# A transformer pair on one Trainium2 core: when the statistic bank is taken again, transposes of first-half weights ahead, and another order for two attention groups

## The chip, the core and the metric

The kernel runs on one core of a Trainium2 chip. The core has five engines with a queue each: TensorE (PE: matmuls, and PEld for its weight loads), VectorE (DVE), ScalarE (ACT), GpSimd (POOL) and SyncE (SP, which issues the DMAs here). Every engine works its own instructions in order; between engines there are semaphores only. The metric is the device time of one launch in microseconds.

## The reference

Two small networks run one after the other on 512 tokens of width 1024, in float32. The first is a block of chunked attention with a relative bias, a gated convolution and an output projection. The second has two layers: sparse top-k attention beside gated linear attention with a squared-ReLU MLP, then stick-breaking attention with another such MLP. The change sits mostly in the stick-breaking layer, whose core is:

```python
def mixer_c(n, w_in, gq, gk, w_out):
    q, k, v = _split(n @ w_in, (C_WIDTH, C_WIDTH, C_WIDTH))
    q = rmsnorm_2(q.reshape(bsz, s_len, N_HEADS_C, HEAD_DIM), gq)   # 8 heads of 128
    k = rmsnorm_2(k.reshape(bsz, s_len, N_HEADS_C, HEAD_DIM), gk)
    ...
    return stick_breaking(q, k, v).reshape(bsz, s_len, C_WIDTH) @ w_out

# stick_breaking, for each head and each block of 128 queries:
    z = q @ k.T * d_h ** -0.5
    lo = where(mask, log_sigmoid(-z), 0.0)
    rc = cumsum(lo, reverse=True)
    a = where(mask, exp(log_sigmoid(z) + (rc - lo)), 0.0)
    out = a @ v
```

## The kernel before

**Precision.** Each float32 matmul operand is split into a high part and a low rest, and three matmuls (high by high, low by high, high by low) add up in one PSUM bank: lines 614 to 616, in `three`. A weight tile (`raw`, 128 x 2048 for each partition row) is split by ACT (line 1401 copies the high part to `wh`) and then by DVE (line 2237 subtracts for `wl`). There are two slots of `raw`, `wh` and `wl`, and `w_lo` counts the finished tiles.

**The stick-breaking layer** is written out by hand as four groups of two heads (`attention_group("stick", g, ...)`, once for each engine) and a closing group 4. Group g projects six blocks from three weight tiles: blocks 0 to 3 are query and key of its two heads (24 matmuls of 512 columns each, banks G0 and G1 in turn), blocks 4 and 5 the values (48 matmuls of 256 columns). Between these blocks PE places the scores, the transposes ("turns") and the products with the values ("av") of the heads of the group before. In group 0 the blocks 0 to 3 run in `first_stick_blocks`, interleaved with the end of the MLP, so that this group has only blocks 4 and 5 left to cover the work of DVE and ACT on its four query and key blocks.

**One query or key block** passes four engines. ACT copies the bank to `tmp` (line 1410) and squares it (line 1418, the high part); POOL makes the exact square (line 2203) and its low rest (line 2208); PE adds over the partitions by two matmuls with ones into the one bank ST (`head_stat`, lines 688 and 689; I call these sums 8 to 23 after their keys); DVE reads ST and makes the mean square (line 2281, `st_x` is raised); ACT takes log, exp and square (lines 1424 to 1426); DVE does a Newton step and scales (lines 2271, 2272, 2772) and raises `st_applied` by a copy of one word (line 2285). `head_stat` waits for the low rest (`sq_low`) and, before the change, for `st_applied` of the sum before it. The copy of block n + 2 into `tmp` waits for `st_applied` of sum n, since there are two buffers.

**The weights of a head** (`weights` on DVE, `softplus` and `exponential` on ACT) come in two halves: score tiles 0 to 2 (banks C0 and C1) and tile 3 (bank C2). ACT: absolute value, exp, log (lines 1718 to 1722); DVE: maximum and add (2829), a reverse scan for each tile (2834), a subtraction (2839), which frees the score bank; ACT: exp (1731), which raises `a_ready`. Then PE transposes ten 128 x 128 pieces into the same three banks (`turns`, line 723), ACT copies them out (1461), POOL masks the diagonals (2197) and PE multiplies by the values (line 1086).

## Time and profile before

| | |
|---|---|
| median of 3 runs | 1581.42 us (1581.22 to 1582.18) |
| profiled execution, its own time | 1582.57 us |
| its span, first to last instruction | 1580.7 us (so 1.9 us lie around it) |
| PE busy | 1561.3 us, 99% |
| DVE, ACT, POOL busy | 1030.1, 725.4, 678.8 us |
| mean granted TensorE clock | 0.998 |

PE is busy nearly all the time; of DVE, ACT and POOL idle time means little except where PE waits for them. In the rows below a timeline row has the start in us from the span's start, the duration in us, engine, line, operation, output and inputs, shape, how many records are merged in it, and in brackets the idle time of the engine before it with what ended that. The duration of a matmul includes its way through the array: unhindered matmuls of 512 columns start 0.23 us apart and last 0.39, so that an idle time in brackets is 0.16 us shorter than what the wait costs (for 256 columns, 0.12 apart and 0.28 long, the same 0.16).

### The profile page before, as it was taken

What the parts mean: (1) busy time and instruction counts of PE and PEld (TensorE: products, weight loads), DVE (VectorE), ACT (ScalarE), POOL (GpSimd) and SP (SyncE); (2) the same over time, 40 slices, a digit from 0 to 9 for tenths busy, and PEclk for the clock granted to TensorE, in tenths of its full rate; (3) what the DMA queues carried; (4) which work ended last, traced back from release to release, by engine and by line L of the source; (5) the groups of instructions that cost most, each with busy time, mean ns of one, the idle gap of its engine ahead of it and who ended that gap; (6) DMA issues with size and microseconds to landing.
All of it is one profiled execution on the core that took longest, in us unless ns stands there. A gap on an engine that the chain in (4) does not pass through costs nothing.

```text
span 1580.7 us, 20565 instructions
## 1 busy us (share of the span) xinstructions
PE 1561.3 (99%) x7578; PEld 1281.5 (81%) x7578; DVE 1030.1 (65%) x1341; ACT 725.4 (46%) x1085; POOL 678.8 (43%) x668
## 2 busy tenths in 40 slices
PE   9999999999999999999999999998999999999999
PEld 7888787787778998888888888777886888888887
DVE  7424554675678977458584848767777557574847
ACT  6323433325245665434353435476765453444433
POOL 0002120104345353285666657432333574857574
PEclk9999999999999999999999999999999999999999
DMA  7232222232311221323233231212120414141321
GB/s 245 80 107 80 80 80 80 96 107 80 104 57 54 93 65 68 136 81 113 101 106 107 82 131 31 99 58 80 54 81 30 158 54 160 53 155 59 134 80 54
DMA packets 25731, 145.07 MB, mean 92 GB/s; under 512 B 3936, under 2 KB 5680, under 8 KB 9264
## 3 DMA queue, kind: packets, MB, share of 16 engines
q1 hardware_dynamic: 25648, 143.95, 26.4%
q8 instruction: 53, 0.87, 0.2%
q14 instruction: 30, 0.25, 0.1%
HBM read 141.84 MB, written 2.10 MB: 91 GB/s over the span
## 4 chain that ended last, share of the span: by engine, by line
PE 84%; DVE 11%; ACT 2%; issue 1%; POOL 1%; ACTq 0%; DVEq 0%; POOLq 0%
PE ps_G L614 19%; PE ps_G L616 18%; PE ps_G L615 18%; PE ps_C L1261 5%; PE ps_C L1259 5%; PE ps_C L1260 5%; DVE wide L2642 1%; DVE top L2638 1%; DVE wide L2834 1%; PE ps_AV L1086 1%; PE ps_AV L1261 1%; PE ps_AV L1259 1%; PE ps_AV L1260 1%; PE ps_C L709 1%; PE ps_C L723 1%
## 5 line engine op out<-in xcount | busy, mean ns | idle before, releaser
L614 PE MATMUL ps_G<-ch,wh 128*128 128x512 f32 x800 | 318.6, 398 | 1.4 <-DVE wl L2237 0.7
L616 PE MATMUL ps_G<-ch,wl 128*128 128x512 f32 x800 | 311.6, 389 | 0.0
L615 PE MATMUL ps_G<-cl,wh 128*128 128x512 f32 x800 | 311.5, 389 | 0.0
L614 PE MATMUL ps_G<-nh,wh 128*128 128x512 f32 x504 | 199.8, 396 | 0.4 <-DVE h L2510 0.2
L2955 DVE TENSOR_TENSOR wl<-raw,wh 128x1024 fp32r<-128x1024 f32 (+1 forms) x104 | 179.7, 1746 | 30.5 <-ACT wh L1899 24.8
L616 PE MATMUL ps_G<-nh,wl 128*128 128x512 f32 x504 | 196.4, 390 | 0.0
L615 PE MATMUL ps_G<-nl,wh 128*128 128x512 f32 x504 | 196.2, 389 | 0.0
L614 PEld LDWEIGHTS ps_G<-ch,wh 128*128 128x128 f32 x800 | 150.2, 188 | 40.1 <-issue 7.1
L615 PEld LDWEIGHTS ps_G<-cl,wh 128*128 128x128 f32 x800 | 150.2, 188 | 33.2 <-issue 2.9
L616 PEld LDWEIGHTS ps_G<-ch,wl 128*128 128x128 f32 x800 | 150.2, 188 | 31.5
L2237 DVE TENSOR_TENSOR wl<-raw,wh 128x2048 fp32r<-128x2048 f32 x46 | 107.3, 2333 | 65.2 <-ACT wh L1401 62.0
L1401 ACT ACTIVATE wh<-raw 128x2048 fp32r<-128x2048 f32 x59 | 112.6, 1908 | 71.8 <-PE ps_G L616 71.8
L1943 ACT ACTIVATE wide<-tmp 128x512 f32<-128x512 f32 x64 | 40.5, 632 | 219.1 <-DVE tmp L2992 218.9
L1259 PE MATMUL ps_C<-wh,nh 128*128 128x512 f32 x320 | 124.6, 389 | 0.0
L1261 PE MATMUL ps_C<-wh,nl 128*128 128x512 f32 x320 | 124.6, 389 | 0.0
L1260 PE MATMUL ps_C<-wl,nh 128*128 128x512 f32 x320 | 124.5, 389 | 0.0
L614 PE MATMUL ps_G<-wh,ch 128*128 128x256 f32 (+1 forms) x400 | 119.1, 298 | 0.0
L2955 DVE TENSOR_TENSOR nl<-wide,nh 128x512 fp32r<-128x512 f32 (+1 forms) x80 | 67.5, 853 | 78.5 <-ACT nh L1947 46.5
L615 PE MATMUL ps_G<-wl,ch 128*128 128x256 f32 (+1 forms) x400 | 115.4, 289 | 0.0
L616 PE MATMUL ps_G<-wh,cl 128*128 128x256 f32 (+1 forms) x400 | 115.4, 289 | 0.0
L614 PEld LDWEIGHTS ps_G<-nh,wh 128*128 128x128 f32 x504 | 94.6, 188 | 25.5 <-issue 5.5
L615 PEld LDWEIGHTS ps_G<-nl,wh 128*128 128x128 f32 x504 | 94.7, 188 | 20.1 <-issue 1.0
(438 smaller groups left out, 3180.9 us busy)
## 6 DMA issues: line engine op xcount, KB each, us to landing
raw<-wst SPq DMA_DIRECT2D x96, 1024.0 KB, 5.0
raw<-quart_d SPq DMA_DIRECT2D x16, 1024.0 KB, 4.9
tabs<-quart_d SPq DMA_DIRECT2D x8, 1024.0 KB, 6.7
mixed_buffers<-quart_d SPq DMA_DIRECT2D x8, 1024.0 KB, 5.5
raw<-wst SPq DMA_DIRECT2D x8, 256.0 KB, 5.9
out<-wide SPq DMA_DIRECT2D x8, 256.0 KB, 2.2
h<-xT SPq DMA_DIRECT2D x7, 256.0 KB, 6.1
raw<-wst SPq DMA_DIRECT2D x2, 512.0 KB, 5.7
```

What stands on the lines that cost most here:

```text
L614: mm(o, ah, bh, start=first, stop=False)
L615: mm(o, ah, bl, start=False, stop=False)
L616: return mm(o, al, bh, start=False, stop=last)
L709: last = mm(ps[b][:, COFF[t]:COFF[t] + w], q[rows, t * P:(t + 1) * P], k[rows, 0:w], start=True, stop=True)
L723: last = nc.tensor.transpose(ps[b][:, TBOFF[j] + (t - j) * P:TBOFF[j] + (t - j + 1) * P], MIX_Sb[side(hd)][:, OFF[t] + j * P:OFF[t] + (j + ...
L1259: mm(o, ah, bh[:, c, :], start=fresh and c == 0, stop=False, skip_group_check=True)
L1260: mm(o, ah, bl[:, c, :], start=False, stop=False, skip_group_check=True)
L1261: return mm(o, al, bh[:, c, :], start=False, stop=c == 3, skip_group_check=True)
L1401: A(wh[s][:], raw[s][:], ACT.Copy).then_inc(w_hi, 1)
L1943: A(wide[:, k, :], tmp[:, k % 2, :], ACT.Square).then_inc(hid_set, 1)
L2237: v.tensor_tensor(wl[s][:], raw[s][:], wh[s][:].bitcast(F), ALU.subtract).then_inc(w_lo, 1)
L2955: return tt(lo, x, hi.bitcast(F), ALU.subtract)
```

## The change

Four things are changed. (1) `head_stat` for the keys ("qk", n), except the first, waits for `st_x` (the mean square has been read from the bank) where it waited for `st_applied` (scaled and applied). (2) `turns` writes the transposes in another order: pieces of tiles 0 to 2 in columns j = 0 and 1 first, then tile 3 of both, then the third bank, whose `take` now stands just ahead of its own transposes. This holds for all turns of the sparse and the stick-breaking groups. (3) In stick groups 0 and 1 the sums stand inside the blocks (`stat_at`), and in group 1 the scores of the second head stand ahead of the av of the first. (4) ACT and DVE work groups 0 and 1 in another order: the tile of values of group 0 is split in halves, the splits of the next tiles stand earlier, and the weights of head 12 have their second softplus half in ACT's list of group 1; in group 1 DVE does the weights of head 13 ahead of the output of head 12.

```diff
             def head_stat(key):
                 q = SQ[key]
-                pe.wait_ge(st_applied, STAT[key])
                 if key[0] == "qk":
                     n = key[1] - 8
+                    if n:
+                        pe.wait_ge(st_x, STAT[key])
+                    else:
+                        pe.wait_ge(st_applied, STAT[key])
                     pe.wait_ge(sq_low, n + 1)
                     mm(ps["ST"][:], ones_r[:], sq_parts[n % 2][0], start=True, stop=False)
                     mm(ps["ST"][:], ones_r[:], sq_parts[n % 2][1], start=False, stop=True).then_inc(sq_used, 1)
                     return
+                pe.wait_ge(st_applied, STAT[key])
...
             def turns(hd, need):
 
-                for b in range(3):
-                    take(("turn", hd, b))
-                for j in range(NT):
+                def turn_(j, t):
+
                     b = MIX[side(hd)][TBANK[j]]
-                    for t in range(j, NT):
+                    return nc.tensor.transpose(
+                        ps[b][:, TBOFF[j] + (t - j) * P:TBOFF[j] + (t - j + 1) * P],
+                        MIX_Sb[side(hd)][:, OFF[t] + j * P:OFF[t] + (j + 1) * P], ident)
+
+                last_t = NT - 1
+                for j in range(2):
+                    take(("turn", hd, j))
+                    for t in range(j, last_t):
                         if j == 0:
                             need(t)
-                        last = nc.tensor.transpose(
-                            ps[b][:, TBOFF[j] + (t - j) * P:TBOFF[j] + (t - j + 1) * P],
-                            MIX_Sb[side(hd)][:, OFF[t] + j * P:OFF[t] + (j + 1) * P], ident)
-                    if j != 2:
-                        last.then_inc(done[b], 1)
+                        turn_(j, t)
+                need(last_t)
+                for j in range(2):
+                    turn_(j, last_t).then_inc(done[MIX[side(hd)][TBANK[j]]], 1)
+                take(("turn", hd, 2))
+                for j in range(2, NT):
+                    for t in range(j, NT):
+                        last = turn_(j, t)
+                last.then_inc(done[MIX[side(hd)][TBANK[last_t]]], 1)
...
                 if first_blocks is not None:
                     first_blocks()
                     head_stat(("qk", qk0))
-                    block_(4, 2, 0)
-                    head_stat(("qk", qk0 + 1))
-                    block_(5, 2, P)
-                    head_stat(("qk", qk0 + 2))
+                    block_(4, 2, 0, stat_at(8, ("qk", qk0 + 1)))
+                    block_(5, 2, P, stat_at(12, ("qk", qk0 + 2)))
                     return
-                block_(0, 0, 0)
                 if name == "stick" and g == 1:
-                    head_stat(("qk", qk0 - 1))
+                    block_(0, 0, 0, stat_at(2, ("qk", qk0 - 1)))
                     block_(1, 0, P)
                     do_turns(0)
-                    block_(2, 1, 0)
-                    head_stat(("qk", qk0))
+                    block_(2, 1, 0, stat_at(1, ("qk", qk0)))
+                    head_stat(("qk", qk0 + 1))
+                    do_scores(1)
+                    do_av(0, prev)
                 else:
+                    block_(0, 0, 0)
                     block_(1, 0, P)
                     head_stat(("qk", qk0))
                     do_turns(0)
                     block_(2, 1, 0)
                     head_stat(("qk", qk0 + 1))
-                if prev is not None:
-                    do_av(0, prev)
-                    do_scores(1)
-                if name == "stick" and g == 1:
-                    head_stat(("qk", qk0 + 1))
+                    if prev is not None:
+                        do_av(0, prev)
+                        do_scores(1)
                 block_(3, 1, P)
                 head_stat(("qk", qk0 + 2))
...
+
+            def split_halves(st, k):
+
+                s = st.slot(k + 1)
+                act.wait_ge(raw_full[s], st.tile_use(k + 1) * 16 + 16)
+                passed(act, done["G1"], st.block_use(2 * k))
+                A(wh[s][:, 0:4, :], raw[s][:, 0:4, :], ACT.Copy).then_inc(second_hi, 1)
+                A(wh[s][:, 4:8, :], raw[s][:, 4:8, :], ACT.Copy).then_inc(w_hi, 1)
...
                 if g == 0:
                     rsqrt(("norm", 4), TOKEN_ROOT)
-                    split(st, 1)
+                    split_halves(st, 1)
                     evac_qk(0, 0)
                     evac_qk(1, 1)
                     rsqrt(("qk", qk0))
+                    split(st, 2)
                     act.wait_ge(rt_set, 2)
                     evac_qk(2, 2)
+                    rsqrt(("qk", qk0 + 1))
                     values_out(wide[:, 12, :], st, 4, 0)
-                    rsqrt(("qk", qk0 + 1))
-                    split(st, 2)
                     evac_qk(3, 3)
+                    rsqrt(("qk", qk0 + 2))
                     values_out(wide[:, 13, :], st, 5, 1)
-                    rsqrt(("qk", qk0 + 2))
-                    weights(hd)
+                    softplus(hd, HALVES[0])
                     return
                 if g == 1:
+                    rsqrt(("qk", qk0 - 1))
+                    softplus(prev, HALVES[1])
+                    split(st, 0)
                     evac_qk(0, 0)
-                    split(st, 0)
-                    rsqrt(("qk", qk0 - 1))
                     exponential(prev)
                     turn(prev)
...
                     newton(("norm", 4), rt, TOKEN_ROOT).then_inc(rt_set, 1)
-                    split(st, 1)
+                    s = st.slot(2)
+                    dve.wait_ge(second_hi, 2)
+                    tt(wl[s][:, 0:4, :], raw[s][:, 0:4, :], wh[s][:, 0:4, :].bitcast(F), ALU.subtract)
+                    dve.wait_ge(w_hi, st.tile(2) + 1)
+                    tt(wl[s][:, 4:8, :], raw[s][:, 4:8, :], wh[s][:, 4:8, :].bitcast(F), ALU.subtract).then_inc(w_lo, 1)
                     apply(0)
-                    apply(1)
+                    apply(1, lambda: split(st, 2))
+                    apply(2)
+
+                    def weights_and_tile():
+                        weights(hd)
+                        split(Step("stick", 1), 0)
+
+                    apply(3, weights_and_tile)
+                    return
+                if not soft and g == 1:
+                    apply(0)
+                    apply(1, lambda: split(st, 1))
+                    weights(prev + 1)
+                    output(prev)
                     split(st, 2)
                     apply(2)
-                    weights(hd, part=0)
-
-                    def rest_and_tile():
-                        weights(hd, part=1)
-                        split(Step("stick", 1), 0)
-
-                    apply(3, rest_and_tile)
+                    apply(3, lambda: output(prev + 1))
                     return
```

Where the instructions stand now, at three places. In the rows `ps_C0` to `ps_C2`, `ps_AV`, `ps_ST` are PSUM banks, `mixed_buffers` holds scores and weights, `tmp` the copies and roots, `nh`, `nl` the squares; the line numbers of the changed kernel are higher.

PE, group 1, the turns of head 12 after block 1 (last matmul of the block, the ten transposes, the first of block 2), with the semaphores waited for. Before:

```order
L616 MATMUL ps_G1<-ch,wl0 128x512
L723 MATMUL ps_C0<-small,mixed_buffers 128x128 [waits moved_C2,a_ready,moved_C1,moved_C0]
L723 MATMUL ps_C0<-small,mixed_buffers 128x128 [waits a_ready] x3
L723 MATMUL ps_C1<-small,mixed_buffers 128x128 x3
L723 MATMUL ps_C2<-small,mixed_buffers 128x128 x3
L614 MATMUL ps_G0<-ch,wh1 128x512 [waits moved_G0,w_lo]
```

Now:

```order
L616 MATMUL ps_G1<-ch,wl0 128x512
L723 MATMUL ps_C0<-small,mixed_buffers 128x128 [waits a_ready,moved_C0]
L723 MATMUL ps_C0<-small,mixed_buffers 128x128 [waits a_ready] x2
L723 MATMUL ps_C1<-small,mixed_buffers 128x128 [waits moved_C1]
L723 MATMUL ps_C1<-small,mixed_buffers 128x128
L723 MATMUL ps_C0<-small,mixed_buffers 128x128 [waits a_ready]
L723 MATMUL ps_C1<-small,mixed_buffers 128x128
L723 MATMUL ps_C2<-small,mixed_buffers 128x128 [waits moved_C2]
L723 MATMUL ps_C2<-small,mixed_buffers 128x128 x2
L614 MATMUL ps_G0<-ch,wh1 128x512 [waits moved_G0,w_lo]
L615 MATMUL ps_G0<-cl,wh1 128x512
L616 MATMUL ps_G0<-ch,wl1 128x512
```

The first transpose waits for C0 and the first half of the weights alone; five transposes stand ahead of the wait for the second half, and C2 is asked for behind seven.

ACT, from the second softplus half of head 12 to its weights, at the seam of groups 0 and 1. Before:

```order
L1722 ACTIVATE mixed_buffers<-mixed_buffers 128x512
L1410 ACTIVATE tmp<-ps_G 128x512
L1418 ACTIVATE nh<-tmp 128x512
L1401 ACTIVATE wh<-raw 128x2048
L1424 ACTIVATE tmp<-tmp 128x512
L1425 ACTIVATE tmp<-tmp 128x512
L1426 ACTIVATE tmp<-tmp 128x512
L1731 ACTIVATE mixed_buffers<-mixed_buffers 128x768
L1731 ACTIVATE mixed_buffers<-mixed_buffers 128x512
```

Now:

```order
L1745 ACTIVATE mixed_buffers<-mixed_buffers 128x768
L1447 ACTIVATE tmp<-tmp 128x512
L1448 ACTIVATE tmp<-tmp 128x512
L1449 ACTIVATE tmp<-tmp 128x512
L1741 ACTIVATE mixed_buffers<-ps_C 128x512
L1744 ACTIVATE mixed_buffers<-mixed_buffers 128x512
L1745 ACTIVATE mixed_buffers<-mixed_buffers 128x512
L1416 ACTIVATE wh<-raw 128x2048
L1433 ACTIVATE tmp<-ps_G 128x512
L1441 ACTIVATE nh<-tmp 128x512
```

The root of sum 11 (three ACTIVATEs of `tmp`) stood behind the copy and square of block 0 and the split of a tile; now it stands ahead of the second softplus half, and the split stands ahead of the copy of block 0.

DVE, group 1, from the split of the values' tile of this group to the weights of head 13. Before:

```order
L2237 TENSOR_TENSOR wl<-raw,wh 128x2048
L2281 SCALAR_TENSOR_TENSOR tmp<-ps_ST,wide 128x512
L2271 SCALAR_TENSOR_TENSOR tmp<-tmp 128x512
L2272 SCALAR_TENSOR_TENSOR tmp<-tmp 128x512
L2772 SCALAR_TENSOR_TENSOR wide<-tmp,par 128x512
L2285 COPY cols<-cols 128x1
L2846 CAST nh<-ps_AV 128x512
L2847 TENSOR_TENSOR nl<-ps_AV,nh 128x512
L2829 SCALAR_TENSOR_TENSOR mixed_buffers<-ps_C,mixed_buffers 128x384 x2
L2834 SCALAR_TENSOR_TENSOR wide<-extra,mixed_buffers 128x128
```

Now:

```order
L2305 SCALAR_TENSOR_TENSOR tmp<-ps_ST,wide 128x512
L2261 TENSOR_TENSOR wl<-raw,wh 128x2048
L2295 SCALAR_TENSOR_TENSOR tmp<-tmp 128x512
L2296 SCALAR_TENSOR_TENSOR tmp<-tmp 128x512
L2796 SCALAR_TENSOR_TENSOR wide<-tmp,par 128x512
L2309 COPY cols<-cols 128x1
L2853 SCALAR_TENSOR_TENSOR mixed_buffers<-ps_C,mixed_buffers 128x384 x2
L2858 SCALAR_TENSOR_TENSOR wide<-extra,mixed_buffers 128x128
L2858 SCALAR_TENSOR_TENSOR wide<-extra,mixed_buffers 128x256
```

The mean square of sum 13 stands ahead of the split where it stood behind it, and the output of head 12 (CAST and its rest) has gone from ahead of the weights of head 13 to behind them.

## Rows read from the trace of the kernel before

**Rows 1.** The page: busy us (share of the span) and instructions of each engine

```profile
PE 1561.3 (99%) x7578; PEld 1281.5 (81%) x7578; DVE 1030.1 (65%) x1341; ACT 725.4 (46%) x1085; POOL 678.8 (43%) x668
```

**Rows 2.** Waits of PE, 960 to 1220 us: us in total, times, longest

```profile
PE ps_C L723 <- DVE mixed_buffers L2839: 4.8, 2, 3.7
PE ps_ST L688 <- DVE cols L2285: 1.5, 2, 0.9
PE ps_ST L688 <- POOL nl L2208: 1.3, 1, 1.3
...
PE ps_G L614 <- DVE wl L2237: 0.7, 1, 0.7
```

**Rows 3.** Timeline of PE in stick groups 0 to 2

```profile
1025.96 0.47 PE L688 MATMUL ps_ST<-nh,ones_r 128*128 128x512 f32 x1 [1.28 <-POOL nl L2208]
...
1052.94 1.41 PE L723 MATMUL ps_C<-small,mixed_buffers 128*128 128x128 f32 x10 [0.31 <-ACT mixed_buffers L1731]
...
1055.03 0.50 PE L614 MATMUL ps_G<-ch,wh 128*128 128x512 f32 x1 [0.68 <-DVE wl L2237]
...
1066.30 0.50 PE L688 MATMUL ps_ST<-nh,ones_r 128*128 128x512 f32 x1 [0.62 <-DVE cols L2285]
...
1073.39 0.50 PE L688 MATMUL ps_ST<-nh,ones_r 128*128 128x512 f32 x1 [0.91 <-DVE cols L2285]
...
1083.58 2.37 PE L723 MATMUL ps_C<-small,mixed_buffers 128*128 128x128 f32 x10 [3.72 <-DVE mixed_buffers L2839]
...
1109.05 1.25 PE L723 MATMUL ps_C<-small,mixed_buffers 128*128 128x128 f32 x10
```

**Rows 4.** Windows: length, busy PE PEld DVE ACT POOL, PEclk, DMA share, GB/s

```profile
1083.50:1085.00 1.50, 1.42 (x7) 1.45 (x8) 1.50 (x1) 1.21 (x3) 0.00 (x0) 0.50 0.00 0
1085.00:1087.00 2.00, 2.00 (x11) 2.00 (x10) 1.25 (x2) 0.69 (x2) 0.00 (x0) 0.50 0.38 53
...
1095.50:1190.00 94.50, 94.50 (x516) 78.80 (x515) 72.81 (x97) 68.93 (x108) 32.13 (x28) 1.00 0.19 67
```

**Rows 5.** Timeline of DVE in stick groups 0 and 1

```profile
1029.41 0.69 DVE L2271 SCALAR_TENSOR_TENSOR tmp<-tmp 128x512 f32<-128x512 f32 x1 [2.02 <-ACT tmp L1426]
...
1031.54 0.15 DVE L2285 COPY cols<-cols 128x1 f32<-128x1 f32 x1
...
1045.25 1.02 DVE L2829 SCALAR_TENSOR_TENSOR mixed_buffers<-ps_C,mixed_buffers 128x384 f32<-128x384 f32 x2 [0.25 <-ACT mixed_buffers L1722]
...
1046.30 1.86 DVE L2834 TENSOR_TENSOR_SCAN wide<-extra,mixed_buffers 128x128 f32<-128x128 f32 x3
...
1052.68 2.29 DVE L2237 TENSOR_TENSOR wl<-raw,wh 128x2048 fp32r<-128x2048 f32 x1
...
1075.63 3.80 DVE L2834 TENSOR_TENSOR_SCAN wide<-extra,mixed_buffers 128x128 f32<-128x128 f32 x3
```

**Rows 6.** Timeline of ACT in stick group 0

```profile
1019.34 1.92 ACT L1401 ACTIVATE wh<-raw 128x2048 fp32r<-128x2048 f32 x1 [1.98 <-PE ps_G L616]
...
1042.60 0.85 ACT L1718 ACTIVATE mixed_buffers<-ps_C 128x384 f32<-128x384 f32 x2
...
1046.40 0.63 ACT L1722 ACTIVATE mixed_buffers<-mixed_buffers 128x512 f32<-128x512 f32 x1
```

**Rows 7.** POOL by source line, 1010 to 1190 us: count, ns min/median/max, starts, forms

```profile
L2203 POOL TENSOR_TENSOR sq<-tmp x16: 1040/1042/2665, 1021.8 to 1172.8; 128x512 f32<-128x512 f32 x16
...
L2208 POOL TENSOR_TENSOR nl<-sq,nh x16: 1262/1297/1562, 1024.6 to 1174.0; 128x512 fp32r<-128x512 f32 x16
```

**Rows 8.** Timeline of POOL in stick groups 0 and 1

```profile
1021.81 2.67 POOL L2203 TENSOR_TENSOR sq<-tmp 128x512 f32<-128x512 f32 x1 [7.41 <-ACT tmp L1410]
...
1077.05 1.56 POOL L2208 TENSOR_TENSOR nl<-sq,nh 128x512 fp32r<-128x512 f32 x1
```

**Rows 9.** Timeline of PE at two turns in other groups

```profile
623.44 0.98 PE L723 MATMUL ps_C<-small,mixed_buffers 128*128 128x128 f32 x7 [0.22 <-POOL mixed_buffers L2042]
...
1206.79 0.79 PE L723 MATMUL ps_ST<-small,mixed_buffers 128*128 128x128 f32 x4 [0.95 <-DVE mixed_buffers L2839]
```

More of the change, by code:

```diff
@@ L1044, in block_, with stat_at @@
                     if k < 4 and name == "stick":
[L1045 removed]
+                        project(st, k, tile, col, mh, ml, each=each)
                     else:
[L1047 to L1048 removed]
+                        project_v(st, k, tile, k % 2, each=each, after=k - 2 if name == "stick" and g == 0 else None)
+                def stat_at(n, key):
+                    return lambda c: head_stat(key) if c == n else None
                 def last_stats(c):
@@ L1139, in attention_group @@
                 if name == "dsa":
[L1140 removed]
+                    block_(0, 0, 0, None if g else last_stats)
                     if g:
```

6 lines of the change are left out of this document (1 added, 5 removed).

## The prediction

> **What bounds the kernel now.** I read the page first: PE is busy for 1561.3 of 1580.7 us [rows 1], so the change can save PE's own instructions, of which it removes none, or PE's waits. The waits of PE name where these are [rows 2]: 4.8 us in two turns behind DVE's subtraction (line 2839), 1.5 us in two sums behind the one-word copy of line 2285, 1.3 us in one sum behind POOL's low rest. The timeline puts nearly all of them in stick groups 0 and 1 [rows 3]; from 1095.5 to 1190 us, the groups 2 and 3, PE is busy for 94.50 of 94.50 us at full clock [rows 4]. So the question is how late DVE, ACT and POOL are in groups 0 and 1, and by how much the new order brings them ahead.
>
> What the waits cost before, each idle time plus 0.16 us for the way through the array: sum 8 at 1025.96, 1.28 + 0.16 = 1.4. Turns of head 12 at 1052.94, 0.31 + 0.16 = 0.5, and the block behind them, which starts 2.09 later where ten transposes need 1.2 (the 1.25 of group 2 less the way through), 0.9. Sum 13 at 1066.30, 0.8 and a slow first pair, 1.0. Sum 14 at 1073.39, 1.1. Turns of head 13 at 1083.58, 3.72 + 0.16 = 3.9 [rows 3]. Together 8.8 us. Behind the last one the granted clock is 0.50 of full [rows 4], that is 1.2 instead of 2.4 GHz, after an idle time of 3.7 us; the turns then take 2.37 instead of 1.25 us [rows 3], and half speed lasts from 1083.6 to 1088.9: 5.35 us for work that needs 3.0 (1.2 of transposes, 15 matmuls at 0.12), 2.3 us lost. All that groups 0 and 1 can give back is 11.1 us.
>
> **What the change does to each, step by step.** Nothing is added but one ACT and one DVE instruction (a tile split in halves, some 0.1 us more on each, beside PE's work), so all depends on when things are ready. I carried the new order through the four engines: each instruction starts when its engine is free and what it waits for has ended, with the durations of the rows. The pieces: the four DVE steps behind a root take 2.3 us (1029.41 to the end of the copy at 1031.69), the weights of a head 6.8 (1045.25 to 1052.68 less 0.6 for a mean square between), a tile 2.29 [rows 5]; on ACT a tile 1.92, the softplus of both halves 4.4 (1042.60 to 1047.03) [rows 6]; on POOL square and rest 1.04 and 1.26 to 1.30 [rows 7]. Roots on ACT take 2.0, by the 2.02 that DVE idles for one [rows 5].
>
> *Collisions.* The first square on POOL, at 1021.81, took 2.67 us, against a median of 1.04 of sixteen [rows 7, 8]: it lasted until 0.9 behind the end of DVE's tile. The three scans that begin at 1075.63 took 3.80 instead of 1.86 [rows 5], while POOL's square and rest ran, the rest itself with 1.56 for 1.26 [rows 8]. So an instruction of DVE with two SBUF inputs and one of POOL don't run at once; one waits for the whole of the other. I count each such meeting at what is left of the earlier one.
>
> The Trainium skill, "SBUF — State Buffer", section "SBUF: two separate sides", says the same: DVE with two SBUF inputs and GpSimd take one port pair by an exclusive lock for the whole instruction. The trace agrees (3.80 for 1.86). It speaks against this change, which puts tiles and Newton steps of DVE beside POOL's squares: without the lock my working has no wait of PE left, and the gain would be 12 us.
>
> *Sum 8.* The tile's first half frees DVE for its second half at 1021.6; that ends at 1022.8 instead of 1023.6, the square 0.9 later, the rest at 1025.0, PE starts near 1025.1: wait 0.6 instead of 1.4.
>
> *Group 0.* Sum 9 now stands in the middle of block 4, which POOL's rest (1027.4) and the mean square (1026.5) precede. Sum 10, twelve steps into block 5, is wanted at 1036.0; its square can't start before 1031.6 and meets the tile that DVE now splits there (1031.3 to 1033.6), so that its rest ends at 1036.1: wait 0.2. That rest meets a Newton step of sum 9, which ends 1.3 later (1037.6), so the copy of block 3 and the scores of head 12 come 0.2 late. Cover gone here costs one for one.
>
> *Turns of head 12.* Softplus starts at 1041.5 instead of 1042.6; the mean square of sum 11 goes ahead of the weights and the weights end at 1050.9 instead of 1052.6. ACT is held by a tile and the copy of block 0, and both halves are ready at 1052.1; PE's transposes begin at 1051.9 and wait for nothing, since five go ahead. The tile behind them is ready at 1053.5: wait 0.25 instead of 0.9. Sum 12, now 3 matmuls into block 2 where it stood behind all 24, needs a rest that POOL can start only behind that tile: 1054.5, wait 0.5. Here the move of the sum makes a wait that was none before.
>
> *Sums 13 and 14* need only the mean square before them (1057.4 and 1063.7), not the copy of line 2285; PE reaches them at 1059.9 and 1069.8. Both waits (1.0 and 1.1) go, 0.1 stays for POOL's rest of 13. ACT and DVE queued behind them are not touched by it: only PE waits there.
>
> *Turns of head 13*, the largest term. Root 12 starts at 1058.0 behind the copy and square of block 1 and ends at 1060.0; DVE's four steps 2.3 + 0.9 for POOL's masks: 1063.1; mean square and tile: 1065.9; root 13 is ready at 1066.4; four steps 2.3 + 1.3 for the square and rest of block 2: 1070.0; weights 6.8 + 0.8 for those of block 3: 1077.6; exponential 0.6: 1078.2. Block 4 ends at 1076.1, five transposes run to 1076.8, and PE waits to 1078.3: 1.5 instead of 3.9. What shortens it is the earlier sum 12 (by 6 us) and the output of head 12 behind the weights (1.4); what is late next is the same chain on DVE. The shorter waits before this one (up to 1.4 us of idle time or so) left the clock at full, so I take the 2.3 us of half clock as gone. Last, the turned weights of head 13 are masked by POOL at 1085.8 while PE is ready at 1085.1: 0.7, new.
>
> **Sum.** New waits 0.6 + 0.2 + 0.2 + 0.25 + 0.5 + 0.1 + 1.5 + 0.7 = 4.1 us, and 0.3 for scores of head 13 now between other work. 11.1 - 4.1 - 0.3 = 6.7 us. The same hand working of the order before gives the turns of head 13 at 1082.2 (really 1083.6), so it is good to about 1.4 us.
>
> *Turns elsewhere.* Where PE waits for tile 3, two more transposes (0.11 us each, from 1.25 for ten) run ahead. That is so at 623.44, after 0.22 idle, and at 1206.79, where the idle 0.95 is for the third bank and the second half comes some 0.4 later [rows 9], and at three more of the kind: 5 x 0.22 = 1.1 us; less than nothing only if the copies of the first bank, which start 0.2 later, were waited for, and av starts behind all three. I take 1.0, bounds 0 and 1.2. Moving the tiles ahead on ACT and DVE asks for weights earlier, but by 7 us at most, and PE never waited for a transfer.
>
> Gain 6.7 + 1.0 = 7.7 us. Against the profiled execution's own 1582.57 us this is 1574.9; that one lies 1.15 over the median of 1581.42, which I don't attribute, so I take the gain from the median: **1573.7 us**.
>
> **Rivals.** *Fewer collisions (12%).* If POOL's squares fall between DVE's steps, the 3.0 us of collisions on the way to the turns of head 13 shrink and the wait of 1.5 goes, with some of the 1.1 in the sums: gain 9 to 12, 1569.5 to 1572.4. For it: the order of two meetings is decided by 0.1 us in my working. Against: a tile of 2.29 and a square wanted inside it meet whatever the order. *The long wait stays long (20%).* The scans lose 1.9 as before instead of my 0.8 [rows 5], the turns wait 2.6, and the clock falls again: 1.1 + 2.3 less, gain 3.6 to 5.5, near 1577. For it: square and scans stand to each other nearly as before. Against: the idle time is cut in two by five transposes, and 2.6 is less than the 3.7 that went ahead of the half clock. *The change doesn't do what it says (6%).* If the sums wait for POOL's rest as long as they did for the copy, the first edit moves the wait's name only, and of group 1 just the reordering is left: 2 to 3 us, about 1579. Against: in my working the rest of 14 is done 1.2 us ahead. *Slower (2%).* DVE becomes the bound of group 1. The gain of 7.7 and 3.2 more would have to be eaten: 10.9, of which the half clock gives 2.3; the remaining 8.6 are seven full meetings of 1.04 to 1.3 us [rows 7] beyond the four or five that I counted, in a stretch where POOL has ten instructions. That decides from about eleven meetings on, and then 1585.
>
> **How the numbers follow.** The forecast, 1572.4 to 1575.5, has 60%. The range leaves out the best of the first rival and the last two: 1571.2 to 1577.6. A difference of 0.2%, 3.2 us, is about what a measurement of this kernel can tell from none. Faster by more than that are the forecast and the first two rivals, 92%; within it 6%; slower 2%.
>
> **What would show it.** In the profile of the changed kernel: no wait of PE behind the one-word copy in sums 13 and 14; a wait of 0.3 to 0.8 at sum 8 and one behind POOL at sum 12; PE at full clock near 1080 us; five transposes of head 13, then an idle time of 1 to 2 us that DVE's line 2839 or ACT's exponential ends; groups 2 and 3 without waits. Wrong would be: an idle time over 2.5 us in these turns, half clock there, or a wait in groups 2 and 3, which would mean that the delay was only passed on.

## The result, and the profile of the changed kernel

The changed kernel takes 1573.94 us (median of 6 runs, 1573.52 to 1574.05), the kernel before, run beside it, 1581.63 us (6 runs, 1581.22 to 1582.23): a ratio of 0.995, 95% interval 0.9938 to 0.9963, 7.7 us less. That is faster by more than 0.2%, and the forecast was 1573.7. The profiled execution took 1573.52 us with a span of 1571.7; it lies 0.4 under its median, that of before 0.9 over its own, so the two profiles differ by 9.05 us, 1.4 more than the medians.

The page: PE's busy time is 3.4 us less than in [rows 1], though it runs the same instructions. Part of that is the stretch at half clock that is gone.

```profile
PE 1557.9 (99%) x7578; PEld 1279.2 (81%) x7578; DVE 1033.1 (66%) x1342; ACT 725.2 (46%) x1086; POOL 682.2 (43%) x668
```

The waits of PE from 1015 to 1215 us (engine, tensor, line, what it waited for: us in total, times, longest), to be laid beside [rows 2]. The waits for the one-word copy have no row any more. Of the 4.8 us in two turns, 3.7 were those of head 13 and are 0.85 now; the other 1.1 is a turn of group 4 that still waits 1.0. So of the 1.8 and 1.1 us left in the turns, 1.0 and 1.1 belong to group 4.

```profile
PE ps_C L723 <- ACT mixed_buffers L1754: 1.8, 2, 1.0
PE ps_ST L723 <- ACT mixed_buffers L1754: 1.1, 1, 1.1
PE ps_ST L691 <- POOL nl L2232: 0.8, 2, 0.5
PE ps_AV L1103 <- POOL mixed_buffers L2221: 0.7, 1, 0.7
```

PE's timeline (start, us, line, tensors, form, count, idle before and what ended it), which answers to [rows 3]: sum 8; turns of head 12 without a wait; the block behind them; sum 12 three matmuls into it; sum 13 straight ahead of the scores of head 13; the turns of head 13 in two halves of five transposes with 0.85 between them; av of head 13 behind POOL's masks.

```profile
1024.22 0.47 PE L691 MATMUL ps_ST<-nh,ones_r 128*128 128x512 f32 x1 [0.52 <-POOL nl L2232]
...
1051.13 1.25 PE L723 MATMUL ps_C<-small,mixed_buffers 128*128 128x128 f32 x10
1052.39 0.50 PE L614 MATMUL ps_G<-ch,wh 128*128 128x512 f32 x1
...
1053.62 0.47 PE L691 MATMUL ps_ST<-nh,ones_r 128*128 128x512 f32 x1 [0.25 <-POOL nl L2232]
...
1058.96 0.39 PE L691 MATMUL ps_ST<-nh,ones_r 128*128 128x512 f32 x1
1059.19 0.39 PE L692 MATMUL ps_ST<-nl,ones_r 128*128 128x512 f32 x1
1059.42 2.32 PE L713 MATMUL ps_C<-wide 128*128 128x128 f32 x8
...
1075.42 0.71 PE L723 MATMUL ps_C<-small,mixed_buffers 128*128 128x128 f32 x5
1076.99 0.77 PE L723 MATMUL ps_C<-small,mixed_buffers 128*128 128x128 f32 x5 [0.85 <-ACT mixed_buffers L1754]
...
1084.69 2.39 PE L1103 MATMUL ps_AV<-mixed_buffers,wide 128*128 128x512 f32 x8 [0.73 <-POOL mixed_buffers L2221]
```

The turns of head 13 and what follows them, the stretch that stood at clock 0.50 in [rows 4], and groups 2 and 3 (stretch, us, PE busy and instructions, granted clock, DMA share, GB/s): full clock in all, and groups 2 and 3 as full as before, so nothing was passed on to them.

```profile
1075.40:1083.50 8.10, 7.25 (x61) 1.00 0.31 93
1083.50:1087.00 3.50, 2.77 (x11) 1.00 0.22 91
1095.50:1181.50 86.00, 86.00 (x479) 1.00 0.21 70
```

Where the 9.05 us lie shows when the same work starts in both timelines:

| start of | before | after | ahead by |
|---|---|---|---|
| turns in the dsa groups, first | 576.8 | 576.2 | 0.6 |
| last av of the dsa groups | 627.0 | 626.0 | 1.0 |
| sum 8 | 1025.96 | 1024.22 | 1.7 |
| turns of head 12 | 1052.94 | 1051.13 | 1.8 |
| scores of head 13 | 1063.35 | 1059.42 | 3.9 |
| turns of head 13 | 1083.58 | 1075.42 | 8.2 |
| scores of head 14 (group 2) | 1095.50 | 1086.92 | 8.6 |
| av of head 18 (group 4) | 1208.07 | 1199.31 | 8.8 |

0.4 us of it is there at 136 us, ahead of anything that was changed. Groups 0 and 1 give 7.6, the transposes in the dsa groups 0.5, group 4 0.2.

### The profile page after: what moved, and what is told of

Its sections match the earlier page's. It is cut to its first block, busy times and chain, and to the rows that moved or that the text cites. A ratio compares the mean times of both kernels' runs of the same rounds, so it can differ in the third digit from the quotient of the medians.

```text
span 1571.7 us, 20555 instructions
## 1 busy us (share of the span) xinstructions
PE 1557.9 (99%) x7578; PEld 1279.2 (81%) x7578; DVE 1033.1 (66%) x1342; ACT 725.2 (46%) x1086; POOL 682.2 (43%) x668
## 4 chain that ended last, share of the span: by engine, by line
PE 83%; DVE 11%; ACT 3%; issue 1%; POOL 1%; DVEq 0%; ACTq 0%; POOLq 0%
PE ps_G L614 19%; PE ps_G L616 18%; PE ps_G L615 18%; PE ps_C L1274 5%; PE ps_C L1276 5%; PE ps_C L1275 5%; DVE wide L2666 1%; DVE top L2662 1%; PE ps_AV L1103 1%; PE ps_AV L1274 1%; PE ps_AV L1276 1%; PE ps_AV L1275 1%; DVE wide L2858 1%; PE ps_C L713 1%; DVE tmp L2295 1%
## 5 line engine op out<-in xcount | busy, mean ns | idle before, releaser
L616 PEld LDWEIGHTS ps_G<-nh,wl 128*128 128x128 f32 x504 | 94.6, 188 | 20.0
```

Source lines behind the costliest of these rows:

```text
L616: return mm(o, al, bh, start=False, stop=last)
```

## Experiments

Times are medians. The kernel before, run beside them, took 1581.4, 1581.7, 1581.3 and 1582.1 us in the four batches; a ratio is the recorded one to before, which isn't exactly the quotient of the two medians. The changed kernel was not run beside the experiments: what is said against it compares medians of different batches, between which the kernel before moved by up to 0.8 us. Where such a difference is small, the profile helps: from sum 8 to the scores of head 14 the kernel before takes 69.5 us and the changed kernel 62.7. Line numbers move by a few where lines were added.

### The new transposes alone

```diff
  (the kernel before)
- def turns: bank by bank, the wait for tile 3 inside the first bank
+ def turns: five transposes of the first half, the wait, then the other five
```

> The kernel before with the new order of transposes alone. My sum gave two more transposes ahead of the wait, 5 x 0.22 = 1.1 us, taken as 1.0, and 0.2 of it again in the turns of head 13: about 1.0 to 1.3 us faster. The trace of after points to less: its PE came 0.5 us earlier out of the first attention groups and gained 0.2 in group 4, which would be 0.7 with nothing for head 13, 0.9 with it. The rival is that nothing is won (below 0.3 us), because the second half of the weights ends the wait whatever ran ahead of it. In the turns of head 13 PE still waits over 3 us and the clock falls to half behind it by every theory.

1579.76 us (1578.21 to 1581.02, 11 runs). The median is 1.6 below that of before, but the ratio is 0.9995 with an interval from 0.9986 to 1.0004, so by the interval the times don't tell it from no change, though all 11 of its runs lie below the median of the 33 before. The trace gives less to the two transposes than my sum: 0.4 us in the dsa groups (turns to last av 49.8 instead of 50.2), 0.2 in group 4. The rest comes from the turns of head 13, which I had not expected:

```profile
1079.58 0.74 PE L719 MATMUL ps_C<-small,mixed_buffers 128*128 128x128 f32 x5 [0.62 <-ACT mixed_buffers L1741]
1081.98 1.33 PE L719 MATMUL ps_C<-small,mixed_buffers 128*128 128x128 f32 x5 [1.67 <-ACT mixed_buffers L1741]
```

and the granted clock there, in PE's windows:

```profile
1079.50:1081.50 2.00, 0.74 (x5) 1.00 0.00 0
1081.50:1084.50 3.00, 2.52 (x12) 0.50 0.00 0
1084.50:1087.00 2.50, 2.50 (x21) 0.91 0.90 295
```

The clock still falls, but it is full again 2.9 us behind the first transpose at half speed, against 5.3 us before, so about 1.2 us less is lost there. Whether the five transposes in the middle of the wait did that is asked again below. The three scans also took 2.66 us here and not 3.80 [rows 5], so that the second half of the turns starts 0.65 us earlier behind sum 8 than the first transpose did before.

### The earlier first reading alone

```diff
  (the kernel before)
- pe.wait_ge(st_applied, STAT[key])
+ pe.wait_ge(st_x, STAT[key])        # all sums but the first of the 16
```

> The kernel before with the first edit alone: sums 9 and later wait for the mean square, not for the one-word copy. By my working the waits of sums 13 and 14 (1.0 and 1.1 us) go, but DVE has the mean square of sum 13 behind a tile, at 1068.4 whenever PE is done, so the weights of head 13 end as late as before: PE waits 2 us longer in the turns of head 13 (idle 5.7 instead of 3.7 us), the clock is half behind it, and the time is the same within 0.4 us. The rival, that each wait is worth its length, gives 2.1 us faster.

1581.98 us (1581.14 to 1583.18, 11 runs), ratio 1.0004 (0.9995 to 1.0013): no change, as the first theory had it. The waits of sums 13 and 14 (1.0 and 1.1 us) are gone and the turns of head 13 wait 1.0 us longer:

```profile
1084.40 2.36 PE L727 MATMUL ps_C<-small,mixed_buffers 128*128 128x128 f32 x10 [4.69 <-DVE mixed_buffers L2843]
```

4.69 instead of 3.72, where I expected 5.7: the chain on DVE ended 1.0 us earlier relative to PE, since the three scans took 2.66 us here and 3.80 in [rows 5]. Both are meetings with POOL, of another length. That the time is still the same comes in part from the clock: none of the 11 executions has a mean granted clock above 0.998, but 45 of the 78 of the kernel before have 0.999 or 1.000. The 33 others of the kernel before, which have 0.998, take 1582.4 us in the median, 0.4 more than this one. So the edit alone gives back a little of the waits and loses it by a longer wait that more often costs the full stretch at half clock.

### The first reading undone in the changed kernel

```diff
  (the changed kernel)
- pe.wait_ge(st_x, STAT[key])
+ pe.wait_ge(st_applied, STAT[key])
```

> The changed kernel with the first edit undone: all sums wait for the one-word copy again. In the new order sum 12 stands ahead of the copy of statistic 11 (1055.5 us) and would wait 2 us, sum 13 (1059.0) for the copy of statistic 12 (1061.8 and later), some 1.3 us more; of these 3.3 us the turns of head 13 give back their wait of 1.0, as the chain on DVE moves less than PE: 2.3 us slower (1.5 to 3.5). The rival, from the first edit being worth nothing by itself: within 0.4 us of the changed kernel.

1578.59 us (1576.71 to 1580.68, 11 runs), 4.7 slower than the changed kernel, twice what I expected. So the same edit is worth nothing in the old order and more than half of the gain in the new one, but these are not the same waits: in the old order it freed sums 13 and 14, here it frees sums 9 and 12, which the new order has moved to where the copy isn't done. I had left sum 9 out: it now stands in the middle of block 4, and with the old wait it stops PE there.

```profile
1030.08 0.80 PE L688 MATMUL ps_ST<-nh,ones_r 128*128 128x512 f32 x1 [2.21 <-DVE cols L2305]
1059.12 0.50 PE L688 MATMUL ps_ST<-nh,ones_r 128*128 128x512 f32 x1 [2.08 <-DVE cols L2305]
```

Behind each of these two waits the clock is half for 3.4 us; of that the windows show:

```profile
1030.00:1033.00 3.00, 2.92 (x11) 0.50 0.00 0
...
1061.00:1064.00 3.00, 3.00 (x9) 0.50 0.00 0
```

The turns of head 13 start 7.1 us later than in the changed kernel and wait for nothing; 2.0 us are given back there and at av of head 13. Four of the 11 executions have a mean clock of 1.000 and take 1576.7 to 1577.3 us, 2.8 to 3.3 more than the changed kernel; so some 1.5 of the 4.7 us is half clock, which my 2.3 had not counted.

### The weights ahead of the output, alone

```diff
  (the kernel before, DVE, stick group 1)
- output(prev)
  weights(prev + 1)
+ output(prev)
```

> The kernel before, with one thing of the new order: DVE in stick group 1 does the weights of head 13 ahead of the output of head 12 (lines 2846 and 2847, 1.4 us). The weights can then start at 1073.5, when the first half of the softplus ends, instead of 1074.6, so the idle time of PE in the turns of head 13 falls from 3.7 to between 2.3 and 2.7 us. If the clock stays at full behind such an idle time, as I took it, the time falls by 1.0 to 1.4 and by the 2.3 us of half clock: 3.3 to 3.7 us faster. If a wait of that length still brings half clock: 1.0 to 1.4 us faster.

1578.65 us (1578.57 to 1580.79, 11 runs), ratio 0.9985 (0.9976 to 0.9994): 2.7 less. The wait falls further than expected, to 0.93 us, because the scans now start ahead of POOL's square and take 1.86 instead of 3.80 us; the clock stays at full. Then a wait comes that was not there: sum 15 for the one-word copy, since the rest of DVE's work in the group is as long as before. Most of what is gained is the clock: nine of the 11 executions have a mean clock of 1.000 and take 1578.6 to 1579.1 us, and the nine such executions of the kernel before 1578.9 to 1579.5.

```profile
1082.42 1.45 PE L723 MATMUL ps_C<-small,mixed_buffers 128*128 128x128 f32 x10 [0.93 <-DVE mixed_buffers L2839]
...
1091.11 0.50 PE L688 MATMUL ps_ST<-nh,ones_r 128*128 128x512 f32 x1 [1.49 <-DVE cols L2285]
```

### Sum 12 late

```diff
  (the changed kernel, PE, stick group 1)
- block_(2, 1, 0, stat_at(1, ("qk", qk0)))
+ block_(2, 1, 0)
+ head_stat(("qk", qk0))
```

> The changed kernel with sum 12 back behind all 24 matmuls of block 2 of stick group 1, where the kernel before has it. By my prediction the early sum 12 is the larger part of what shortened the wait in the turns of head 13. The mean square of 12 would then come near 1059.5 instead of 1055.5 us and the Newton steps near 1061.8 instead of 1058.8, so the chain on DVE ends some 3.0 us later; sum 13, which waits for that mean square, is held by 1 us; PE's own work is 0.4 ahead since sum 12 waits for nothing. Idle time in the turns of head 13: 2.5 to 3.5 us, and half clock behind it as behind 2.1 us and more elsewhere. In all 4 to 5.5 us slower than the changed kernel, 2.5 to 3 if the clock stays at full. The rival, that the weights' place ahead of the output was what counted and the chain starts elsewhere: under 1 us.

1577.23 us (1576.62 to 1579.33, 11 runs), 3.3 slower than the changed kernel; I expected 4 to 5.5 with half clock.

```profile
1077.66 0.74 PE L723 MATMUL ps_C<-small,mixed_buffers 128*128 128x128 f32 x5 [1.22 <-ACT mixed_buffers L1755]
1080.06 0.83 PE L723 MATMUL ps_C<-small,mixed_buffers 128*128 128x128 f32 x5 [1.67 <-ACT mixed_buffers L1755]
```

and PE's window behind it:

```profile
1081.00:1084.00 3.00, 3.00 (x16) 0.50 0.00 0
```

The chain is late by 2.8 us: the second five transposes start at 1080.06 instead of 1076.99, less 0.3 by which the whole stretch is later at sum 8. The clock falls, but costs some 1.6 us and not 2.3, and av of head 13 gives its 0.9 back; that is what I counted too high. The early sum 12 is worth 3.3 of the 7.6 us of groups 0 and 1; from sum 8 to the scores of head 14 this profile takes 66.0 us where the changed kernel takes 62.7, which is 3.3 too.

### A tile done twice

```diff
  (the changed kernel, DVE, inside the statistic of sum 13)
+ step(tt(wl[s][:], raw[s][:], wh[s][:].bitcast(F), ALU.subtract))
  split(st, 1)
```

> The changed kernel, with DVE doing the tile subtraction of 2.28 us at 1062.5 twice, ahead of the Newton steps of sum 13. The chain to the turns of head 13 is late by 1.9 us (0.4 of it fits in an idle time), so PE's idle time there grows from 0.9 to about 2.8 us. If the clock stays at full behind it: 1.9 us slower than the changed kernel. If it falls to half, as behind the 3.7 us of the kernel before: 1.9 + 2.3 = 4.2 us slower. If DVE were not what the turns wait for: no change. In groups 2 and 3 nothing waits by any of these.

1578.73 us (1577.45 to 1579.11, 11 runs), 4.8 slower. PE's waits in the turns of head 13 are 2.25 and 1.67 us, and the clock falls behind them:

```profile
1078.14 0.74 PE L723 MATMUL ps_C<-small,mixed_buffers 128*128 128x128 f32 x5 [2.25 <-ACT mixed_buffers L1754]
1080.54 0.87 PE L723 MATMUL ps_C<-small,mixed_buffers 128*128 128x128 f32 x5 [1.67 <-ACT mixed_buffers L1754]
```

```profile
1081.00:1084.00 3.00, 3.00 (x17) 0.51 0.00 0
```

The sum is near the 4.2 expected, its parts are not: 2.28 us of work made the chain 3.2 us late (1080.54 to 1076.99, less 0.3), since the second subtraction took 3.01 us, a Newton step 1.78 and the scans 3.57 beside POOL. The Newton steps together were 0.3 us shorter than in the changed kernel; so the added work made two meetings longer and one shorter, and the chain lost 1 us by it.

### The same with one wait

```diff
  (the kernel of the last experiment)
- def turns: five transposes, the wait, then the other five
+ def turns: as in the kernel before, all three banks taken first
```

> The changed kernel with the tile subtraction done twice, and the transposes in the old order, which takes all three banks before the first transpose. PE then waits once in the turns of head 13, for 4.4 to 4.7 us, where with the new order it waits 2.25 and 1.67 us with five transposes between. With the new order the clock was half for 3.4 us. If transposes in the middle of the wait are what made it short, half clock lasts 6 to 7 us here, as in the kernel before and in the one with the first edit alone (4.7 us of idle time), and the time is 1.0 to 1.5 us higher than with the new order for the clock, 0.7 for the five transposes behind the wait and 0.4 to 0.7 for the turns elsewhere: 1580.8 to 1581.6. If the length of the half clock has nothing to do with them, it is 3.4 us again and the time 1579.8 to 1580.1.

1579.18 us (1578.39 to 1580.47, 11 runs), 0.45 more than the last one; both theories expected more. The kernel before was 0.4 higher beside this run than beside the last one, so the two times show no difference. The profile is that of the first theory: one wait, and half clock from 1078.8 to 1085.6, 6.8 us, against 3.4 us (1081.1 to 1084.5).

```profile
1080.45 2.37 PE L727 MATMUL ps_C<-small,mixed_buffers 128*128 128x128 f32 x10 [4.15 <-DVE mixed_buffers L2853]
```

```profile
1079.00:1085.50 6.50, 5.05 (x24) 0.50 0.12 16
```

These two profiles differ by 1.5 us, the medians by 0.45. The profiled execution with two waits had a mean clock of 0.999, but 7 of its 11 executions had 0.998, as 8 of 11 have here. A mean of 0.999 is one stretch of 3.4 us, 0.998 one of 6.8, if there is no other in the execution. So by these means the short stretch isn't owed to the transposes alone: the kernel before, which has none in its wait, has 0.999 in 36 of 78 executions and 0.998 in 33. Whether the new order makes it more frequent stays open; with the new transposes alone 1 of 11 executions had 0.998.

### POOL's work cut to 8 columns

```diff
  (the changed kernel, POOL, sums 12 to 15)
- g.tensor_tensor(whole, tmp[:, n % 2, :], tmp[:, n % 2, :], ALU.mult)
+ g.tensor_tensor(whole[:, 0:8], tmp[:, n % 2, 0:8], tmp[:, n % 2, 0:8], ALU.mult)
  (and the rest, line 2232, in the same way)
```

> The changed kernel with POOL's squares and low rests of sums 12 to 15 cut from 512 to 8 columns each (their low parts are left out, so these statistics are a little off). By the theory of an exclusive turn between DVE with two SBUF inputs and POOL: the Newton steps at 1052.3 and 1066.2 fall from 1.77 and 1.67 to 0.69 us, the three scans of head 13 from 2.65 to 1.85, sum 12 waits for nothing, the weights of head 13 end 2 to 3 us earlier and PE waits less than 0.2 us in the turns of head 13: 1.3 to 1.5 us faster than the changed kernel. By the rival, that these DVE instructions were slow for a reason other than POOL: they stay as long as they were, only the wait of sum 12 goes: 0.4 us faster.

1572.04 us (1571.39 to 1572.57, 5 runs), 1.9 less than the changed kernel. The turns of head 13, sum 12 and av of head 13 wait for nothing; the last, 0.9 us, was not in my 1.3 to 1.5. From sum 8 to the scores of head 14 it takes 60.1 us. Two rows of DVE's timeline and two of POOL's:

```profile
1060.76 2.28 DVE L2262 TENSOR_TENSOR wl<-raw,wh 128x2048 fp32r<-128x2048 f32 x1
...
1067.00 1.85 DVE L2859 TENSOR_TENSOR_SCAN wide<-extra,mixed_buffers 128x128 f32<-128x128 f32 x3
```

```profile
1060.95 2.15 POOL L2228 TENSOR_TENSOR sq<-tmp 128x8 f32<-128x8 f32 x1 [3.15 <-ACT tmp L1433]
1063.18 0.20 POOL L2233 TENSOR_TENSOR nl<-sq,nh 128x8 fp32r<-128x8 f32 x1
```

The scans are at 1.85 again, 2.65 in the changed kernel; both Newton steps that had taken 1.77 and 1.67 are at 0.69. The clearest row is POOL's square of 8 columns: 0.20 us of work, 2.15 us long, until DVE's tile of the same moment ends. Here it doesn't share, it waits.

### A tile with one SBUF input

```diff
  (the changed kernel, DVE, two tiles of stick group 1)
- v.tensor_tensor(wl[s][:], raw[s][:], wh[s][:].bitcast(F), ALU.subtract)
+ ts(wl[s][:], raw[s][:], 0.0, None, ALU.mult)
```

> The changed kernel, with the two tile subtractions of DVE at 1050.0 and 1062.5 replaced by a multiplication of one SBUF input by zero, of the same 128x2048 (the low parts of these two tiles are left out). If only DVE instructions with two SBUF inputs shut POOL out, POOL's rest at 1050.3 falls from 3.20 to 1.3 us and its square at 1062.7 from 2.99 to 1.04. If any DVE instruction on SBUF does, they last to the end of the tile as before. If the one-input form is shorter than 2.3 us, the chain to the turns of head 13 is that much earlier and its wait of 1.0 us and that of sum 12 go: up to 1.5 us faster.

1572.24 us (1571.14 to 1573.46, 4 runs), 1.7 less than the changed kernel. The first condition is refuted in this form: the instruction with one input shuts POOL out too.

```profile
1062.92 1.22 DVE L2267 TENSOR_SCALAR wl<-raw 128x2048 fp32r<-128x2048 f32 x1
```

```profile
1063.11 1.92 POOL L2227 TENSOR_TENSOR sq<-tmp 128x512 f32<-128x512 f32 x1 [2.11 <-ACT tmp L1433]
```

POOL's square of 1.04 us starts at 1063.11 and takes 1.92: the tile's end at 1064.1 and 0.9 more. The multiplication does 2048 columns in 1.22 us where the subtraction needs 2.28, so it does about two columns in the time of one. The Trainium skill, "SBUF — State Buffer", section "SBUF: two separate sides", names both cases, two SBUF inputs or a mode that uses two ports, as holders of the same lock; the two rows agree with it, and my "two SBUF inputs" was too narrow. The gain isn't the shorter instruction as such: behind the tile DVE now idles 1.44 us for the root of sum 13 where it idled 0.38. It comes from shorter meetings behind it.

```profile
1065.58 1.37 DVE L2301 SCALAR_TENSOR_TENSOR tmp<-tmp 128x512 f32<-128x512 f32 x1 [1.44 <-ACT tmp L1449]
...
1069.49 1.85 DVE L2864 TENSOR_TENSOR_SCAN wide<-extra,mixed_buffers 128x128 f32<-128x128 f32 x3
```

The two Newton steps take 1.37 and 0.69 us (1.07 and 1.67 in the changed kernel) and the scans 1.85 (2.65). POOL's rest for sum 12, which meets the other tile, takes 2.13 instead of 3.20, and its wait goes as well. From sum 8 to the scores of head 14 it takes 60.3 us.

### A meeting moved

```diff
  (the changed kernel, ACT, stick group 1)
+ split(st, 2)
  evac_qk(3, 3)
- split(st, 2)
```

> The changed kernel, with ACT splitting the tile (line 1416) ahead of its copy of block 3 in group 1, so that POOL's square and rest of sum 15 come 1.9 us later, behind the three scans of head 13 instead of beside them. By the exclusive turn of DVE and POOL the scans fall from 2.65 to 1.85 us; the scan of 512 may meet the square instead and lose up to 0.5. The exponential of the first half would wait for ACT up to 0.3 us. PE's wait in the turns of head 13 falls from 1.0 to between 0.2 and 0.7: 0.3 to 0.8 us faster than the changed kernel. The rival, that such meetings are only moved, gives no change.

1573.94 us (1573.70 to 1574.08, 5 runs): exactly the changed kernel. The three scans take 1.86, as hoped, and the scan of 512 columns takes 1.91 instead of 1.22, because POOL's rest now meets that one. PE's wait is 0.74 instead of 0.85.

```profile
1070.14 1.86 DVE L2861 TENSOR_TENSOR_SCAN wide<-extra,mixed_buffers 128x128 f32<-128x128 f32 x3
...
1073.94 1.91 DVE L2861 TENSOR_TENSOR_SCAN wide<-extra,mixed_buffers 128x512 f32<-128x512 f32 x1
```

### The copies ahead of a root, and everything at once

```diff
  (the changed kernel, ACT, stick group 1)
+ turn(prev + 1)
  rsqrt(("qk", qk0 + 2))
- turn(prev + 1)
```

> The changed kernel, with ACT copying the turned weights of head 13 (line 1484) ahead of the root of sum 14, which waits for DVE's mean square at 1079.8. POOL's masks, which begin at 1083.5 behind these copies, can then begin near 1079.5, and the root starts at 1080.5 as before, since ACT idles 2.9 us ahead of it. The wait of av of head 13 (0.9 us) goes: 0.9 us faster than the changed kernel. The rival is that groups 2 and 3, fed by the same engines, hold PE back by as much: no change.

1573.21 us (1572.57 to 1573.86, 5 runs), 0.7 less than the changed kernel, no more than batches differ by; the profile decides it. POOL's masks begin at 1079.75, av of head 13 waits for nothing, and from sum 8 to the scores of head 14 it takes 61.8 instead of 62.7 us.

```diff
  (that, the tile ahead of the copy of block 3, and on PE)
- head_stat(("qk", qk0)); block_(4, 2, 0, stat_at(8, ...))
+ block_(4, 2, 0, two_stats)          # sum 8 six matmuls in, sum 9 as before
- block_(2, 1, 0, stat_at(1, ("qk", qk0)))
+ block_(2, 1, 0, stat_at(2, ("qk", qk0)))
```

> The changed kernel with what is left of the waits attacked at once: sum 8 stands six matmuls into block 4, sum 12 three further matmuls into block 2, ACT splits the tile ahead of its copy of block 3, and copies the turned weights ahead of the root of sum 14. Waits that should go: sum 8 0.7, sum 12 0.4, av of head 13 0.9, of the turns of head 13 0.3 to 0.8 as in the run with that alone. 2.3 to 2.8 us faster than the changed kernel, near 1571.3. If waits ahead are only passed on to the turns of head 13, whose end DVE sets, the 1.1 us of the two sums are lost there again, and 1.2 to 1.7 remain.

1572.80 us (1572.60 to 1574.98, 5 runs), 1.1 less than the changed kernel, the fastest of those that leave nothing out, though its runs overlap those with the copies alone. The second case of the expectation came about. Sums 8 and 12 wait for nothing, but sums that come a little later hand on what they saved:

```profile
PE ps_ST L691 <- POOL nl L2241: 1.0, 2, 0.8
PE ps_C L723 <- ACT mixed_buffers L1758: 0.7, 1, 0.7
```

Its chain on DVE stands where it stood. Only av of head 13, which has no chain behind it, is a clean gain: from the turns of head 12 to the scores of head 14 it takes 34.8 us, 34.9 with the copies alone and 35.8 in the changed kernel.

No run takes the split tile of group 0 or ACT's new order alone; what they give is read from the timelines only.

## Why the prediction was right, point by point

**The waits.** Each is idle time plus 0.16 as in the prediction. Sum 8: 0.6 predicted, 0.68 measured. Sum 10: 0.2 and 0.2. Scores of head 12: 0.2 and 0.1. The tile behind the turns of head 12: 0.25 and 0.26. Sum 12: 0.5 and 0.42, behind POOL as predicted. Sum 13: 0.1 and 0. Turns of head 13: 1.5 and 1.0. Av of head 13: 0.7 and 0.9. Together 3.6 us against 4.1. The 0.3 for scores between other work isn't seen. So groups 0 and 1 gave 7.6 instead of 6.7 us.

One term of the working was read wrong: ten transposes were taken as 1.2 us, but the block behind those of group 2, which start at 1109.05 [rows 3], starts 1.01 later:

```profile
1110.06 0.47 PE L614 MATMUL ps_G<-ch,wh 128*128 128x512 f32 x1
```

So the tile behind the turns of head 12 cost 1.1 and not 0.9 before, and the half clock about 2.5 and not 2.3 (5.35 us less 1.0 for the transposes and 1.8 for 15 matmuls).

**The chain to the turns of head 13.** Its rows, on ACT and DVE:

```profile
1058.12 0.63 ACT L1449 ACTIVATE tmp<-tmp 128x512 f32<-128x512 f32 x1
```

```profile
1062.48 2.28 DVE L2261 TENSOR_TENSOR wl<-raw,wh 128x2048 fp32r<-128x2048 f32 x1
...
1066.24 1.67 DVE L2296 SCALAR_TENSOR_TENSOR tmp<-tmp 128x512 f32<-128x512 f32 x1
...
1069.72 2.65 DVE L2858 TENSOR_TENSOR_SCAN wide<-extra,mixed_buffers 128x128 f32<-128x128 f32 x3
...
1075.58 0.69 DVE L2863 TENSOR_TENSOR mixed_buffers<-ps_C,wide 128x512 f32<-128x512 f32 x1
```

Root 12 ends at 1058.75 (predicted 1060.0), the tile at 1064.76 (1065.9), the copy of sum 13 at 1068.8 (1070.0), the weights at 1076.27 (1077.6). All are 1.1 to 1.3 us early because the first is; from there on the durations are those of the working. The scans lose 0.8 us to POOL, as put in. PE itself reached the turns 0.8 us earlier than predicted, which leaves 0.5 less wait.

**The half clock.** It is gone and was worth about what I gave it. That can be seen without a change of code: of 78 executions of the kernel before, 9 have a mean granted clock of 1.000 and take 1578.9 to 1579.5 us (median 1579.1), the 69 others 1579.8 to 1583.6. So at full clock the change is worth 5.2 us (1579.1 to 1573.9; the prediction's terms without the clock give 5.4), and the rest of the 7.7, 2.5, is the clock.

**The turns elsewhere** are the term that was mis-sized: 5 x 0.22 us, taken as 1.0, and 0.7 in the trace, 0.5 in the dsa groups and 0.2 in group 4. There the second half of the weights was already nearly ready, and what ran ahead did not all lie in a wait.

**Errors that cancel.** That the 7.7 us came out exact is luck. The sum had 0.9 too little for groups 0 and 1 and 0.3 too much for the turns, which leaves 0.6; the profiles have 0.4 more at their start and 0.3 elsewhere, for which there was no term. Together that is the 9.05 us of the profiles, and the medians differ by 1.4 less.

**The rivals.** A longer wait that keeps the half clock didn't come, but my argument against it was weak. I held 2.6 us of idle time for harmless since 3.7 had gone ahead of the half clock; the kernel with the first reading undone shows half clock behind 2.1 and 2.2, though not in each of its executions. The changed kernel, at 0.85, was safe by the length of its wait and not by that argument. The slower case would have needed seven meetings more; the tile done twice shows that one tile brings about one.

## What to carry to other kernels

An edit that takes waits away from the engine that is the bound is worth only what the chain behind the next wait allows: alone the earlier reading gave nothing. In the order that moved that chain taking it out cost 4.7 us, because sums had been placed that rely on it. So find the chain (here root, Newton steps, weights on ACT and DVE) and put its first link, a sum, as early as its input allows; where that takes a sum into the middle of a block, its wait must be of the earliest kind. Count as a cost each pair of DVE and POOL instructions that would run at once. A reordering can dissolve such a meeting (with the weights ahead of the output the scans fell from 3.80 to 1.86 us) or only move it (with the tile ahead they fell from 2.65 to 1.86 and the next one rose from 1.22 to 1.91): measure the chain's end.

## What the runs showed of the hardware that I had not expected

- The clock falls sooner than the kernel before let one think. Idle times of PE of 2.08 and 2.21 us were followed by half clock, as were 3.72, 4.15 and 4.69, and pairs with five transposes between (0.62 and 1.67, 1.22 and 1.67, 2.25 and 1.67); 0.85, 0.93 and 1.49 were not. It doesn't follow in every execution. A mean clock of 1.000 had 9 of 78 executions of the kernel before (3.72), none of 11 each with 4.15, 4.69 and 2.25 and 1.67, 5 of 11 with 1.22 and 1.67, 4 of 11 with 2.21 and 2.08, 9 of 11 with 0.93 and 1.49, and all 6 of the changed kernel.
- A stretch at half clock lasted either 3.4 us (five cases, PE at work in nearly all of it) or 6.8 (three cases, PE idle in its first 1.1 to 1.6 us). Half of the part in which PE worked is lost: an estimate of 1.5 to 1.7 us for the short ones and 2.6 to 2.9 for the long ones, where the wait lasted on into the half clock.
- In the profiles of two of the kernels (the first reading alone, the output late) the clock was half for 3.4 us, from 482.5 and 482.3 us, where nothing was changed and PE was busy throughout, and PE was some 1.5 us late behind it. So a mean below 1.000 need not come from the wait, as in the profiled execution of the output late (0.999). What decides when it falls stays open. The rows are of the first reading alone; their 0.82 and 0.75 are means over 4 us:

```profile
480.00:484.00 4.00, 4.00 (x26) 0.82 0.00 0
484.00:488.00 4.00, 4.00 (x13) 0.75 0.34 86
```

- A POOL instruction of 8 columns took 2.15 instead of 0.20 us beside a DVE subtraction; a DVE instruction with one SBUF input at twice the speed holds POOL off as well.
